# Index stage of a decode step: two samples' products in 32-column strips, seven gather buffers, keys copied in place

## What is computed

```python
def index_scores(q_idx, w_idx, k_idx):
    dots = jnp.einsum('bqhd,bkd->bqhk', q_idx, k_idx).astype(jnp.float32)
    return jnp.einsum('bqhk,bqh->bqk', jax.nn.relu(dots), w_idx.astype(jnp.float32)) * IDX_SCALE

def dsa_sample(q, kv_new, q_idx, w_idx, k_idx_new, cache_kv, cache_idx, page_table, rel_bias):
    ...
    kidx_past = cache_idx[page_table].reshape(b, past, IDX_DIM)          # 8 samples x 2048 keys x 64
    sc = jnp.where(..., index_scores(q_idx, w_idx, kidx_all), -jnp.inf)
    _, sel = lax.top_k(sc, n_sel)                                         # 256 of 2049 keys a sample
    ...

def dsa_prompt(q, k, v, q_idx, w_idx, k_idx, rel_bias):                   # 4 blocks of 128 queries
    sc = jnp.where(k_pos <= q_pos, index_scores(qi_b, w_b, k_idx), -jnp.inf)
    _, sel = lax.top_k(sc, n_sel)                                         # 128 of up to 512 keys a query
    return dsa_attend(...)
```

## Time and profile before

| | us |
|---|---|
| median of 3 runs | 1165.07 |
| lowest, highest | 1163.37, 1166.27 |
| the profiled execution | 1163.57 |
| its span, first to last instruction | 1161.8 |
| PE busy | 1125.1 (97%) |
| DVE, ACT, POOL busy | 686.5, 398.9, 101.6 |

### The profile page before, as it was taken

One profiled execution on the slowest core, in us unless ns is written; L12 is line 12 of the kernel. 1 busy time (PEld: TensorE's weight loads), 2 busy tenths in 40 slices (PEclk: granted clock), 3 DMA queues, 4 the chain that ended last, 5 costly groups with the idle time before them and its releaser, 6 DMA issues.

```text
span 1161.8 us, 22104 instructions
## 1 busy us (share of the span) xinstructions
PE 1125.1 (97%) x9038; PEld 983.1 (85%) x9038; DVE 686.5 (59%) x1541; ACT 398.9 (34%) x758; POOL 101.6 (9%) x155
## 2 busy tenths in 40 slices
PE   7999999898998999999999999899999999999998
PEld 5898886465575899999989777589999999999998
DVE  4545844979787587778886634545454545453440
ACT  4522323622577755555555424521011101000000
POOL 3100002001106300000000111100000000000000
PEclk9999999978999999999999999999999999999999
DMA  9997651022011202222213377513333333252341
GB/s 322 270 279 183 197 147 55 1 73 82 28 32 52 82 2 82 83 83 83 83 32 114 138 254 254 212 44 91 90 90 91 92 92 93 73 141 76 100 121 28
DMA packets 141874, 129.15 MB, mean 111 GB/s; under 512 B 17635, under 2 KB 135824, under 8 KB 139712
## 3 DMA queue, kind: packets, MB, share of 16 engines
q1 hardware_dynamic: 137184, 86.78, 25.4%
q0 software_dynamic: 4608, 41.23, 9.7%
HBM read 124.58 MB, written 3.41 MB: 110 GB/s over the span
## 4 chain that ended last, share of the span: by engine, by line
PE 85%; DVE 7%; ACT 3%; issue 2%; DMA 2%; POOL 0%; ACTq 0%; DVEq 0%; POOLq 0%
PE psV L1290 22%; PE psV L1033 15%; PE psA L1290 11%; PE psA L673 9%; PE psV L1158 4%; PE psV L946 3%; PE psA L1013 2%; PE psV L705 2%; PE psV L804 2%; PE psA L1083 2%; PE psV L969 1%; PE psA L955 1%; DMA r<-cache_idx,rows_of 1%; PE psV L714 1%; PE psA L1123 1%
## 5 line engine op out<-in xcount | busy, mean ns | idle before, releaser
L1033 PE MATMUL psV<-r_r,wide_r 128*128 128x260 f32 x1536 | 207.7, 288 | 2.8 <-DVE msk L2243 2.2
L1033 PEld LDWEIGHTS psV<-r_r,wide_r 128*128 128x128 f32 x1536 | 190.4, 189 | 5.3 <-issue 3.5
L1586 ACT ACTIVATE wring<-psV 128x512 f32<-128x512 f32 x128 | 76.3, 597 | 92.9 <-PE psV L1033 70.5
L1290 PE MATMUL psV<-qiz_r,wring_r 128*128 128x260 f32 x528 | 93.9, 283 | 0.0
L2444 DVE TENSOR_TENSOR wide<-wide,psV 128x520 f32<-128x520 f32 x22 | 15.3, 697 | 126.6 <-PE psV L1290 126.6
L2244 DVE TENSOR_REDUCE msk<-wring 128x8 f32<-128x512 f32 x128 | 86.4, 676 | 0.0
L1290 PEld LDWEIGHTS psV<-qiz_r,wring_r 128*128 128x128 f32 x528 | 76.2, 188 | 0.0
L673 PE MATMUL psA<-wide_r,wring_r 128*128 128x260 f32 x416 | 76.0, 285 | 0.0
L1290 PE MATMUL psA<-qiz_r,wring_r 128*128 128x260 f32 x352 | 70.9, 283 | 0.0
L1290 PE MATMUL psA<-qiz_r,r_r 128*128 128x260 f32 x352 | 70.9, 282 | 0.0
L1290 PE MATMUL psA<-hT_r,r_r 128*128 128x260 f32 x352 | 70.8, 283 | 0.0
(11 more groups left out here) (568 smaller groups left out, 2504.9 us busy)
## 6 DMA issues: line engine op xcount, KB each, us to landing
wring<-w_ffn_in SPq DMA_DIRECT2D x44, 512.0 KB, 3.7
wide<-w_ada SPq DMA_DIRECT2D x11, 1024.0 KB, 7.4
wring<-w_ffn_out SPq DMA_DIRECT2D x16, 704.0 KB, 4.6
tok<-w_ada SPq DMA_DIRECT2D x9, 1024.0 KB, 5.4
wring<-w_in SPq DMA_DIRECT2D x24, 256.0 KB, 5.9
wring<-w_out SPq DMA_DIRECT2D x8, 512.0 KB, 5.8
wide<-w_out SPq DMA_DIRECT2D x2, 2048.0 KB, 7.9
r<-w_ada SPq DMA_DIRECT2D x3, 1024.0 KB, 10.7
```

Source lines behind the costliest of these rows:

```text
L1033: mm = pe.matmul(kx[m % 2][:, hf, :], w, wtab[:, b % 2, l, 2 * k + hf, :], start=(k == 0 and w is high and l == 0), stop=(k == 1 and w is ...
L1290: mm = pe.matmul(out[:, hf, 0:HT], w[:, k, :], x[:, hf * HT:(hf + 1) * HT], start=(k0 + k == 0 and x is xh and w is high), stop=(k0 + k == ...
L1586: A(sq2[m % 2].rearrange("p (x n) -> p x n", x=2), kx[m % 2][:, :, 0:256], ACT.Square).then_inc(kx_squared, 1)
```

## The change

- The 32 columns of the stationary matrix that a sample's queries lie in are used alone: `w1[:, b * 128:(b + 1) * 128][:, r]`, r being one of four strips. Samples are taken in the order 0, 2, 1, 3, 4, 6, 5, 7, and the products of two samples that lie in different strips are issued together, behind the third, fifth, seventh and eighth turn (`IDX_SETS`).
- A whole sample (8 transposes, 1024 columns, both banks of a slot) is turned and copied at a time, and ScalarE writes it back over the rows that were gathered.
- There are seven buffers: the two of `ip`, four in `qiz`, one in `r1[:, 0:1024]`. The first two gathers wait for `rows_of` and `g8`, the next five for the copies out of `qiz` into `w1` and for one product (`queries_ready` 4, `new_ready` 1), the eighth for the fourth turn.
- For that, VectorE computes `rows_of` earlier (behind `tab_loaded`), and clears and fills `w1` and the first 64 columns of `irel` directly behind `g8`. Six rounds follow there instead of eight, then seventeen instead of fifteen, and eight in the index stage instead of sixteen. `ROUND_AT` has units 1, 3, ... 29 and 41, 44, 47.
- `copy_group` goes from VectorE to ScalarE, at the same units, behind the unit's exponential; the eighth stands at the start of the samples' attention.

```diff
-        A_IP = nA; nA += 16
+        A_IP = nA; nA += NB
...
-        ip = r1[:, 3848:5896].rearrange("p (s n) -> p s n", s=2)
-        kiT = r1[:, 0:1024].rearrange("p (s n) -> p s n", s=2)
+        idx_flat = qiz[:].rearrange("p a t -> p (a t)")
+        idx_slots = [r1[:, 3848:4872], r1[:, 4872:5896]] + [idx_flat[:, x * 1024:(x + 1) * 1024] for x in range(4)] + [r1[:, 0:1024]]
+        IDX_ORDER = (0, 2, 1, 3, 4, 6, 5, 7)
+        IDX_SETS = {2: (0, 1), 4: (2, 3), 6: (4, 5), 7: (6, 7)}
...
-        pages_in = [sem(f"pages_in{x}") for x in range(2)]
-        IDX_IN = 16 * NB // 2
-        kv_rows = [sem(f"kv_rows{x}") for x in range(3)]
+        pages_in = [sem(f"pages_in{x}") for x in range(7)]
+        IDX_IN = (32, 16)
...
-            pe.wait_ge(queries_ready, 1)
+            pe.wait_ge(queries_ready, 5)
...
-            pe.wait_ge(new_ready, 2)
+            pe.wait_ge(new_ready, 1)
...
-            def idx_product(n):
-                b, g = divmod(n, 2)
-                pe.wait_ge(a_free, A_IP + n + 1)
-                return pe.matmul(sv(V_IS)[:, g, :], w1[:, b * 128:(b + 1) * 128], kiT[:, n % 2, :], start=(b == 0), stop=(b == 7),
-                                 skip_group_check=True)
-            for x in range(17):
-                if x < 16:
-                    b, g = divmod(x, 2)
-                    pe.wait_ge(pages_in[b % 2], 16 * (b // 2 + 1))
-                    pe.wait_ge(a_free, A_IP + x - 1)
-                    for y in range(4):
-                        c = g * 512 + y * 128
-                        mm = pe.transpose(sa(A_IP + x)[:, 0, y * 128:(y + 1) * 128], ip[:, b % 2, c:c + 128], ident)
-                    mm.then_inc(a_full, 1)
-                if x == 1:
-                    pe.wait_ge(v_free, V_IS - 1)
-                if x >= 1:
-                    mm = idx_product(x - 1)
+            def idx_products(at):
+                pe.wait_ge(a_free, A_IP + max(at) + 1)
+                for g in range(2):
+                    for x in at:
+                        b = IDX_ORDER[x]
+                        r = slice(32 * (b // 2), 32 * (b // 2) + 32)
+                        mm = pe.matmul(sv(V_IS)[r, g, :], w1[:, b * 128:(b + 1) * 128][:, r], idx_slots[x % 7][:, g * 512:(g + 1) * 512],
+                                       start=(b % 2 == 0), stop=(b % 2 == 1), skip_group_check=True)
+                return mm
+            pe.wait_ge(v_free, V_IS - 1)
+            for x in range(NB):
+                pe.wait_ge(pages_in[x % 7], 16 * (x // 7 + 1))
+                pe.wait_ge(a_free, A_IP + x - 1)
+                out = sa(A_IP + x).rearrange("p b n -> p (b n)")
+                for y in range(8):
+                    mm = pe.transpose(out[:, y * 128:(y + 1) * 128], idx_slots[x % 7][:, y * 128:(y + 1) * 128], ident)
+                mm.then_inc(a_full, 1)
+                if x in IDX_SETS:
+                    mm = idx_products(IDX_SETS[x])
...
-            for n in range(16):
-                act.wait_ge(a_full, A_IP + n + 1)
-                A(kiT[:, n % 2, :], sa(A_IP + n)[:, 0, :], ACT.Identity).then_inc(a_free, 1)
+            for x in range(NB):
+                act.wait_ge(a_full, A_IP + x + 1)
+                A(idx_slots[x % 7], sa(A_IP + x).rearrange("p b n -> p (b n)"), ACT.Identity).then_inc(a_free, 1)
...
+                if u >= 13 and u % 8 == 5 and u < NA:
+                    copy_group(act, u // 8 - 1)
...
+            copy_group(act, 7)
+
+        def copy_group(act, x):
+            act.wait_ge(pv_done, 8 * x + 8)
+            nc.scalar.activation(oS[x % 2], psV[:, x % 2, 1, :], ACT.Identity).then_inc(o_copied, 1)
...
+            v.tensor_scalar(rows_of[:], ptab[:], 8.0, sel[:, 80:81], ALU.mult, ALU.add).then_inc(rows_ready, 1)
...
-            ROUND_AT = list(range(1, 20, 2))
+            ROUND_AT = list(range(1, 30, 2)) + [41, 44, 47]
-            for _ in range(8):
+            link(v.memset(w1, 0.0))
+            w1v = w1.rearrange("p (b x) -> p b x", x=144)
+            for p0, c in ((0, 0), (64, 8)):
+                for odd in range(2):
+                    v.tensor_copy(w1v[p0:p0 + 64, :, c + odd:c + 8:2],
+                                  qiz[odd * 64:odd * 64 + 64, odd:8:2, SEQ:T].rearrange("p h b -> p b h")).then_inc(queries_ready, 1)
+            v.tensor_tensor(irel[:, 0:64].rearrange("p (h b) -> p h b", h=H), qiz[:, :, SEQ:T],
+                            kidxT[:, SEQ:T].unsqueeze(1).broadcast_to([128, H, NB]), ALU.mult).then_inc(new_ready, 1)
+            for _ in range(6):
...
-            v.wait_ge(tab_loaded, 160)
-            v.tensor_scalar(rows_of[:], ptab[:], 8.0, sel[:, 80:81], ALU.mult, ALU.add).then_inc(rows_ready, 1)
-            link(v.memset(w1, 0.0))
-            w1v = w1.rearrange("p (b x) -> p b x", x=144)
-            for p0, c in ((0, 0), (64, 8)):
-                for odd in range(2):
-                    v.tensor_copy(w1v[p0:p0 + 64, :, c + odd:c + 8:2],
-                                  qiz[odd * 64:odd * 64 + 64, odd:8:2, SEQ:T].rearrange("p h b -> p b h")).then_inc(queries_ready, 1)
-            for _ in range(15):
+            for _ in range(17):
...
-            v.tensor_tensor(irel[:, 0:64].rearrange("p (h b) -> p h b", h=H), qiz[:, :, SEQ:T],
-                            kidxT[:, SEQ:T].unsqueeze(1).broadcast_to([128, H, NB]), ALU.mult).then_inc(new_ready, 1)
...
-            for _ in range(16):
+            for _ in range(8):
...
-            def copy_group(x):
-
-                v.wait_ge(pv_done, 8 * x + 8)
-                v.tensor_copy(oS[x % 2], psV[:, x % 2, 1, :]).then_inc(o_copied, 1)
-
...
-                if u >= 13 and u % 8 == 5:
-                    copy_group(u // 8 - 1)
...
-            copy_group(7)
...
-            for b in range(NB):
-                if b >= 2:
-                    g.wait_ge(a_full, A_IP + 2 * b - 2)
-                fetch(ip[:, b % 2, :], "cache_idx", IDX, b, pages_in[b % 2])
+            for x in range(NB):
+                if x == 2:
+                    g.wait_ge(queries_ready, 4)
+                    g.wait_ge(new_ready, 1)
+                if x == 7:
+                    g.wait_ge(a_full, A_IP + 4)
+                fetch(idx_slots[x % 7], "cache_idx", IDX, IDX_ORDER[x], pages_in[x % 7])
-            kv_rows_of = lambda b, s: fetch(kvp[s].rearrange("p j n -> p (j n)"), "cache_kv", 256, b, kv_rows[s])
+            kv_rows_of = lambda b, s: fetch(kvp[s].rearrange("p j n -> p (j n)"), "cache_kv", 256, b, pages_in[2 + s])
```

## The result

| us | kernel before | changed kernel |
|---|---|---|
| median (19 runs each) | 1167.54 | 1174.20 |
| lowest, highest | 1163.37, 1174.46 | 1170.07, 1176.94 |
| the profiled execution | 1163.57 | 1173.60 |
| its span | 1161.8 | 1171.8 |

The ratio is 1.0055 (95% interval 1.0037 to 1.0072). The forecast was 1169.7, +6.1 us on the profiled execution of before. The time itself lies 0.7 us above the end of the range, and the two profiled executions are 10.0 us apart, not 6.1.

A forecast was written before the change was run, and what follows sets the result against it. TensorE fills 97% of the span on average, but each of four changed stretches has its own limit. Terms -10.2 + 5.6 + 1.6 + 5.5 + 2.2 + 1.4 = +6.1 us on 1163.57 gave 1169.7; range 1162.0 to 1173.5.

The forecast's parts named there:

- The index stage (-10.2): Index stage: paired strips side by side, hidden gathers and an earlier start end it at 289.5 instead of 299.7 us.
- the 1.5 us that the prediction left in it for a low clock: Index stage: 3 us at half clock, as at 274 to 277 us before, were left in, costing 1.5 us.
- The load (+5.6): Bias rows' load ahead of the index stage: seven early gathers delay it, so TensorE's line 859 starts 5.6 us later.
- By packets, the load got one for two: Transfer queues, earlier trace: 72 load packets against 146 gather packets; so at most a fifth for the load while gathers queue.
- The prediction's sentence on the Trainium skill: Transfer queues: by the skill's packet rule, many 1 KB load pieces travel against 4 KB rows, getting half the bandwidth or more.
- The clock behind that gap (+1.6): TensorE's line 859 after the load's wait: first 3 us at half clock, +1.6 us, bounds 0 and 3.3.
- Units 16 to 31 (+5.5): Attention units 14 to 31: six new 1.51 us rounds overfill VectorE and TensorE waits, +5.5 us.
- Units 32 to 63 (+2.2 and +1.4): Attention units 32 to 63: late rounds cost 2.2 us, output copies waiting behind ScalarE's exponential 1.4 us.
- The base and the range: Whole kernel: terms added to the profiled 1163.57 us, 1.5 below the median; range 1162.0 to 1173.5.
- Rival 1: Bias rows' load: with half the bandwidth it delays TensorE 1.6 us without clock dip; +0.5, 1164.1 us; chance 0.24.
- Rival 2: Attention: rounds fall into VectorE's idle time and moved copies give back 5.5 us; -8.5, 1155.1 us; chance 0.12.
- Rival 3: Index stage: strips don't run side by side, a sample pair takes 3.44 instead of 1.85; +6.4, 1176.1 us; chance 0.06.

The follow-up runs named there:

- Experiment 4: Changed kernel with each index product taken over all 128 output columns again instead of in strips: 1178.02 us, ratio 1.0104 to the kernel before.
- 5: Changed kernel with all gathers held until the bias rows have landed: 1169.57 us, ratio 1.0014 to the kernel before.
- 11: Changed kernel with all gathers held behind the bias rows' load and the output copies back on VectorE: 1165.77 us, ratio 0.9983 to the kernel before.
- 1: Changed kernel with the third and later gathers held until the bias rows have landed: 1170.61 us, ratio 1.0029 to the kernel before.
- 2: Changed kernel with eight of the last sixteen selection rounds left out (output incomplete): 1162.17 us, ratio 0.9955 to the kernel before.
- 3: Changed kernel with the attention outputs' copies back on VectorE, behind the unit's rounds: 1170.71 us, ratio 1.0027 to the kernel before.
- 10: Changed kernel with 56 extra TensorE transposes filling its gaps in units 16 to 29: 1171.17 us, ratio 1.0021 to the kernel before.
- 8: Kernel before with only the copies of the attention outputs moved to ScalarE: 1167.72 us, ratio 0.9998 to the kernel before.
- 7: Kernel before with only the changed kernel's placing of the selection rounds: 1182.63 us, ratio 1.0113 to the kernel before.

## Why the prediction was right and wrong

**The index stage (-10.2): right, with two errors that cancel.** 27.88 to 17.73 us, -10.15, with no wait for a gather and products of 1.91 us for the 1.85 taken from the earlier trace rows. Experiment 4 shows that the strips are 6.5 of it. Each pair of samples took 4.05 us instead of 3.83 (a turn is 1.04 instead of 0.9), and the stage is 0.8 longer than worked out for full clock. But the 1.5 us that the prediction left in it for a low clock didn't come: the clock was 1.00. Of the forecast 10.2, 0.8 was the earlier start, which the table counts in the stretch before (26.7 and 26.8 us in 5 and 11 for 27.4).

**The load (+5.6): too large, right in mechanism.** It landed after 10.2 us (11 to 13 forecast), and TensorE's first product with `trev` came 3.5 us later. The step that failed in this term is the reading of the earlier trace rows: "By packets, the load got one for two". That stretch showed a load with 0.04 MB in 5 us; here it got 0.46 MB in three. Experiments 1 and 5 show the cause, since the landing falls to 8.1 and 5.8 as gathers are taken from ahead of it. The prediction's sentence on the Trainium skill went wrong too: it gave the load many pieces for each row of the gathers, where the rule counts descriptors alike for both queues.

**The clock behind that gap (+1.6): about right on average, too small in this execution.** The stretch to the transposes took 4.3 us more, at 0.58. TensorE waited for the load in all six kernels with early gathers, for 2.8 to 5.2 us. Its products behind the gap then took 6.76, 5.40 and 5.40 us in three of them (the changed one, 1 and 2), and 3.70, as at full clock, in the other three (3, 4 and 10). Over the six the stretch took 28.5 us on average (26.6 to 31.7), over the seven kernels that don't wait so long 27.3 (26.7 to 28.9): 1.2 us, within the bounds of 0 and 3.3, and smaller than the scatter. Load and clock together come to 7.8 us in this execution, for 7.2 forecast, and to 4.7 on average.

**Units 16 to 31 (+5.5): right.** +6.5 measured; the copies on ScalarE cost 0.9 there on their own (8). Experiment 2 takes 5.7 of it away. VectorE full there, with 1.51 us for each new round, was the reading of the earlier trace rows.

**Units 32 to 63 (+2.2 and +1.4): wrong in size, by a term that the sum didn't have.** +6.5 measured. The rounds (1.7) and the copies (0.8) came out below the forecast. The other 4.0 us are put down to TensorE at half clock from 341 to 358 us. The prediction had a clock term behind the gap of the load and none behind the gaps that it forecast itself, with "TensorE ... waits" in units 14 to 31. That is the step of the mechanism that failed: I had argued that TensorE waits where VectorE is full, and counted that only as time. Experiment 10 shows the link from the gaps to the clock.

**The sum.** With the clock term missing the attention was forecast 3.9 us too low (9.1 for 13.0), and load and clock at the front 2.5 us too high on average (7.2 for 4.7). These two cancel for the most part; that the medians are 6.7 apart, for 6.1 forecast, is so far luck.

**The base and the range: this put the time outside.** The terms were added to the profiled execution, 1163.57, said to lie 1.5 us below the median and inside the spread of 2.9. Three runs showed too little of the spread: over 19 runs the median is 1167.54 and the spread 11.1 us. The profiled execution had a mean clock of 0.987; the median of the kernel before is 0.981 in each of three sets of 29 runs, and in these a clock lower by 0.01 goes with 7 to 9 us more, so the 0.006 stand for 4 to 5 us. With 6.1 on 1167.54 the forecast would have been 1173.6. The range was made of the mechanisms' bounds alone, and had nothing for this.

**The rivals.** Rival 1 (the load gets its share) was half right: near half of the bytes at first, then a sixth, and a delay of 3.5 us for its 1.6. Rival 2 (VectorE relieved, rounds free) falls with 2 and 8: the late rounds cost 10.9 us with the clock that they bring down, and the copies taken from VectorE gave nothing in the kernel before. Rival 3 (strips not side by side) falls with 4.

Still open is why the clock stays low for so long in some kernels with late rounds (the changed one, 1, 4, 5 and 7: 0.53 to 0.71 in units 32 to 47) and only briefly in 3 and 11 (0.92 and 0.98). It is not a draw of single executions: the median of the mean clocks over all runs is 0.968, 0.972, 0.971, 0.970 and 0.969 in those five, 0.978 and 0.980 in 3 and 11. The copies on ScalarE go with it in four of the five, but 7 has them on VectorE.

## What to carry over

Place filling work by the single gaps of its engine, not by the idle sum of a stage, and where it makes TensorE wait, allow for the price of the half clock beside that of the wait. A gather started early can delay a load that the critical chain waits for, as here by 4 to 5 us; start it behind that load. Before a forecast of half a per cent, ask how far the profiled execution lies from a typical one: here its mean clock told.

## What I had not expected of the hardware

Most of this kernel's spread between runs goes with the granted clock. In the 29 runs of the kernel before beside experiment 1 it lies between 0.970 and 0.989, the times between 1160.7 and 1176.9, with a correlation of -0.92. Part of it falls in stretches in which the kernels do the same, as in units 0 to 7 (13.87, 15.55 or 17.23 us) and before `g8`.

Useless work cost nothing and may have paid: with 56 transposes added to a stretch in which TensorE waits, the clock held, and the median came out 0.34% lower, at the edge of what the measurement can tell.
